# A two-layer hybrid trunk in fp32 on one core: the start reordered with small filler products, and the LRU gate products cut into 64x64 quarters

## What is computed

```python
for l in range(DEPTH):                         # DEPTH = 2
    xn = rmsnorm(x, pre_mix_g[l])
    u, g, q, k, v, gA, gB = split(xn @ w_in[l])
    # branch A: conv of width 4, then the gates of a linear recurrence
    uc = conv_b + sum(upad[:, k:k + S] * conv_w[k] for k in range(4))
    ub = uc.reshape(B, S, 16, 64)                              # 16 blocks of 64 channels
    r = sigmoid(einsum("bsnd,nde->bsne", ub, w_a) + b_a)       # a 64x64 matrix for each block
    i = sigmoid(einsum("bsnd,nde->bsne", ub, w_x) + b_x)
    h = scan(a=exp(-8 * r * softplus(-lam)), b=sqrt(1 - a*a) * i * uc)
    y_a = (h * gelu(g)) @ w_pa[l]
    # branch B: rotary, windowed attention with sinks, then @ w_pb[l]
    x = x + rmsnorm((sigmoid(gA) * y_a + sigmoid(gB) * y_b) @ w_o[l], post_mix_g[l])
    f = (silu(h @ w_ffn_gate[l]) * (h @ w_ffn_up[l])) @ w_ffn_down[l]    # h = rmsnorm(x, pre_ffn_g[l])
    x = x + rmsnorm(f, post_ffn_g[l])
```

## Time and profile before

| | |
|---|---|
| median of 3 runs | 822.87 us (822.86 to 823.91) |
| the profiled execution's own time | 823.39 us |
| span of its trace | 821.6 us |
| PE busy | 808.5 us, 98% of the span |
| DVE busy | 537.7 us, 65% |
| ACT busy | 419.5 us, 51% |
| POOL busy | 69.2 us, 8% |
| DMA | 148.07 MB, mean 180 GB/s |

### The profile page before, as it was taken

How to read it: one execution, slowest core, us unless ns; L and a number is a source line. 1 busy time by engine, 2 the same in 40 slices (tenths; PEclk the granted TensorE clock), 3 DMA queues, 4 the chain that set the end, 5 groups by cost and what they waited for, 6 DMA issues and landing times.

```text
span 821.6 us, 10326 instructions
## 1 busy us (share of the span) xinstructions
PE 808.5 (98%) x4221; PEld 683.9 (83%) x4221; DVE 537.7 (65%) x549; ACT 419.5 (51%) x543; POOL 69.2 (8%) x131
## 2 busy tenths in 40 slices
PE   7999999999999999999999999999999999999997
PEld 4898898888888888888879989988888888888885
DVE  5798898556666464545488869975467645645652
ACT  5556878633455343434345588865336434443431
POOL 7331000000120000000011300000003100000000
PEclk9999999999999999999999999999999999999999
DMA  9875545354358566654448735444454466655511
GB/s 280 262 256 157 160 162 184 119 184 164 108 200 279 175 213 204 198 164 151 154 132 274 276 131 186 155 154 154 158 199 153 169 218 208 201 179 187 198 52 51
DMA packets 80016, 148.07 MB, mean 180 GB/s; under 512 B 7137, under 2 KB 27745, under 8 KB 79970
## 3 DMA queue, kind: packets, MB, share of 16 engines
q1 hardware_dynamic: 79552, 147.40, 54.3%
q10 hardware_dynamic: 418, 0.02, 0.0%
HBM read 146.36 MB, written 1.05 MB: 179 GB/s over the span
## 4 chain that ended last, share of the span: by engine, by line
PE 97%; DVE 1%; DMA 1%; issue 0%; ACT 0%; POOL 0%; SPq 0%; DVEq 0%; POOLq 0%; ACTq 0%
PE work L636 17%; PE work L638 17%; PE work L637 17%; PE acc L636 9%; PE acc L638 9%; PE acc L637 9%; PE work L628 4%; PE work L630 4%; PE work L629 4%; PE work L770 1%; PE acc L701 1%; PE work L724 1%; DMA weights_raw<-in_w_in 1%; PE acc L714 1%; PE work L733 1%; PE work L734 1%
## 5 line engine op out<-in xcount | busy, mean ns | idle before, releaser
L1302 DVE TENSOR_TENSOR weights_lo<-weights_raw,weights_hi 128x2048 fp32r<-128x2048 f32 x132 | 301.7, 2290 | 156.1 <-ACT weights_hi L946 156.1
L946 ACT ACTIVATE weights_hi<-weights_raw 128x2048 fp32r<-128x2048 f32 x132 | 252.5, 1915 | 210.9 <-PE work L638 118.8
L636 PE MATMUL work<-weights_hi,act_a_hi 128*128 128x512 f32 x544 | 214.4, 394 | 0.0
L638 PE MATMUL work<-weights_hi,act_a_lo 128*128 128x512 f32 x544 | 212.1, 390 | 0.0
L637 PE MATMUL work<-weights_lo,act_a_hi 128*128 128x512 f32 x544 | 211.9, 389 | 0.0
L638 PEld LDWEIGHTS work<-weights_hi,act_a_lo 128*128 128x128 f32 x544 | 102.1, 188 | 21.4
L636 PEld LDWEIGHTS work<-weights_hi,act_a_hi 128*128 128x128 f32 x544 | 102.2, 188 | 21.0
L637 PEld LDWEIGHTS work<-weights_lo,act_a_hi 128*128 128x128 f32 x544 | 102.2, 188 | 20.5
L636 PE MATMUL acc<-weights_hi,act_b_hi 128*128 128x512 f32 x240 | 94.3, 393 | 0.0
L638 PE MATMUL acc<-weights_hi,act_b_lo 128*128 128x512 f32 x240 | 93.5, 390 | 0.0
L637 PE MATMUL acc<-weights_lo,act_b_hi 128*128 128x512 f32 x240 | 93.4, 389 | 0.0
(11 more groups left out here) (182 smaller groups left out, 895.9 us busy)
## 6 DMA issues: line engine op xcount, KB each, us to landing
weights_raw<-in_w_in SPq DMA_DIRECT2D x43, 1024.0 KB, 5.3
weights_raw<-in_w_ffn_down SPq DMA_DIRECT2D x22, 1024.0 KB, 4.9
weights_raw<-in_w_ffn_gate SPq DMA_DIRECT2D x20, 1024.0 KB, 5.2
weights_raw<-in_w_ffn_up SPq DMA_DIRECT2D x20, 1024.0 KB, 5.1
weights_raw<-in_w_pa SPq DMA_DIRECT2D x8, 1024.0 KB, 5.0
weights_raw<-in_w_pb SPq DMA_DIRECT2D x8, 1024.0 KB, 5.0
weights_raw<-in_w_o SPq DMA_DIRECT2D x8, 1024.0 KB, 4.8
weights_raw<-in_w_ffn_gate SPq DMA_DIRECT2D x4, 512.0 KB, 4.0
```

The costliest lines, as they stand in the source:

```text
L636: mm(dst, xh, wh, start=first, stop=False)
L638: return mm(dst, xl, wh, start=False, stop=final)
L946: activate(w_hi[:, SLOT[n], :], raw[:, n % RAW, :], ACT.Copy).then_inc(hi_done.sem, 1)
L1302: v.tensor_tensor(w_lo[:, SLOT[n], :], raw[:, n % RAW, :], bits(w_hi[:, SLOT[n], :]), ALU.subtract).then_inc(split_done.sem, 1)
```

## The change

The start: DVE's cast of the positions goes from the head of its order to a place behind the x tiles' work; the loads of positions and sinks go from ACT's queue to SP's, behind the third panel; ACT copies the turned x tile before it splits the second half of the first panel; POOL makes the second rstd right behind the first, ahead of the angle chain, and clears nothing; PE multiplies the identity by itself 5 times and 8 times (`keep_busy`), into a bank that nobody reads; the turning of `vec_rows` goes between two kv panel halves.

The gates: both 64x64 matrices of a block are stored side by side in `gate_w` (half the room, nothing to clear), and a group takes four fp32 products of 64 rows by 64 columns of weights, 256 columns moving. The r products of both halves go straight (rows b to output partitions b) into one bank, the i products crosswise into the other, so two groups share two banks. ACT reads r with one sigmoid for each group, i with two of 64 partitions, crosswise; `lru_bx` is loaded crosswise to fit.

```diff
@@ SP
-                                      lru_bx.rearrange("l (k b) e -> (l k) (b e)", b=2),
+                                      None,
+                    for b in range(2):
+                        sp.dma_start(vec_rows[row:row + DEPTH * KD, 64 - 64 * b:128 - 64 * b],
+                                     lru_bx.rearrange("l (k b) e -> b (l k) e", b=2)[b]).then_inc(rows_loaded, 16)
             load(0, 2)
+            sp.dma_start(pos_i[:, :], positions.rearrange("a (t p) -> p (a t)", p=P), ...
+            sp.dma_start(sink_rows[:, :, :], attn_sinks.rearrange("l h -> (l h)").partition_broadcast(P) ...
...
-                        sp.wait_ge(*cleared.at(l, 2))
+                        if not first:
+                            sp.wait_ge(*x_done.at(l - 1, 4))
@@ POOL
-            nc.gpsimd.memset(bd_a, 0.0).then_inc(cleared.sem, 1)
-            nc.gpsimd.memset(bd_x, 0.0).then_inc(cleared.sem, 1)
             steps[0] += 1
             rstd_of(0, (ms_done.sem, 1), steps[0])
+            steps[0] += 1
+            rstd_of(1, (ms_done.sem, 2), steps[0])
@@ PE
+            def keep_busy(n):
+                for _ in range(n):
+                    nc.tensor.transpose(work[3][:, 0:P], ident[:, :], ident[:, :])
+            keep_busy(WARM[0])
...
+            keep_busy(WARM[1])
@@ PE, gates
-                    for c in range(c0, c1):
-                        dst = claim(l, "gates", c)
-                        pe.wait_ge(*uc_done.at(l, c + 1))
-                        mm(dst[:, 0:S], bd_a[:, c, :], UC[:, c, :], start=True, stop=True)
-                        mm(dst[:, S:2 * S], bd_x[:, c, :], UC[:, c, :], start=True, stop=True
-                           ).then_inc(gates_mm.sem, 1)
+                    for pair in range(c0, c1, 2):
+                        dsts = [claim(l, "gates", c) for c in (pair, pair + 1)]
+                        pe.wait_ge(*uc_done.at(l, pair + 2))
+                        for c in (pair, pair + 1):
+                            cols = slice(S * (c - pair), S * (c - pair) + S)
+                            for i in range(2):
+                                for b in range(2):
+                                    rows = slice(64 * b, 64 * b + 64)
+                                    to = 64 * b if i == 0 else 64 - 64 * b
+                                    last = mm(dsts[i][to:to + 64, cols], gate_w[rows, c, 64 * i:64 * i + 64],
+                                              UC[rows, c, :], start=True, stop=True)
+                        last.then_inc(gates_mm.sem, 1)
@@ PE, first_products
-                    pe.wait_ge(rows_loaded, 16 * 5)
-                    nc.tensor.transpose(acc[:, 1, 0:P], vec_rows[:, :], ident[:, :]).then_inc(vec_turned, 1)
+                        if j == 0:
+                            pe.wait_ge(rows_loaded, 16 * 6)
+                            nc.tensor.transpose(acc[:, 1, 0:P], vec_rows[:, :], ident[:, :]).then_inc(vec_turned, 1)
@@ ACT
-            act.dma_start(pos_i[:, :], ...
-            act.dma_start(sink_rows[:, :, :], ...
             half_hi(0, 0).then_inc(head_hi, 1)
+            xa_hi(0, 0, "xn", 0)
             act.wait_ge(*raw_loaded[0].at(0, LOADED[0]))
             half_hi(0, 1).then_inc(hi_done.sem, 1)
-            xa_hi(0, 0, "xn", 0)
@@ DVE
-            dve.wait_ge(pos_loaded, 16)
-            v.tensor_copy(pos_f[:, :], pos_i[:, :]).then_inc(pos_done, 1)
...
-            xa_lo(0, 0, "xn", 0, range(1))
+            xa_lo(0, 0, "xn", 0)
             dve.wait_ge(*hi_done.at(0, 1))
             half_lo(0, 1).then_inc(split_done.sem, 1)
-            xa_lo(0, 0, "xn", 0, range(1, 2))
...
             xa_lo(0, 0, "xn", 1)
+            dve.wait_ge(pos_loaded, 16)
+            v.tensor_copy(pos_f[:, :], pos_i[:, :]).then_inc(pos_done, 1)
```

More of the change, by code:

```diff
@@ L40 @@
 GELU_SCALE = 0.7978845608028654
+WARM = (5, 8)
 RAW = 3
@@ L181, in trunk @@
         thA = QTOK
-        bd_a, bd_x = (QT[:, k:k + 4, :].rearrange("p a (b d) -> p (a b) d", b=2) for k in (0, 4))
+        gate_w = QT[:, 0:4, :].rearrange("p a (b d) -> p (a b) d", b=2)
         junk = KTOK[:, :, :, :].rearrange("p t g d -> p (t g d)")
@@ L413, in layer @@
                     if n == RAW:
[L415 removed]
+                        if not first:
+                            sp.wait_ge(*x_done.at(l - 1, 4))
                         for b in range(2):
[L417 to L418 removed]
+                            for i, src in enumerate((lru_wa, lru_wx)):
+                                sp.dma_start(gate_w[64 * b:64 * b + 64, :, 64 * i:64 * i + 64],
                                              src[l].rearrange("(k b) d e -> b d k e", b=2)[b]
[L420 removed]
+                                             ).then_inc(gate_w_loaded.sem, 16)
                     if n == 4 + RING + RAW:
@@ L531, in _ @@
                     less(n - m, 1 + m)
-                if n == 0:
-                    steps[0] += 1
-                    rstd_of(1, (ms_done.sem, 2), steps[0])
             for n, piece in ((2, 1), (1, 2), (0, 3), (2, 2), (1, 3), (2, 3)):
@@ L563, in layer @@
                         rstd_of(n, ms_done.at(l, m + 1), l * 10 + step)
-                if not last:
-                    pool.wait_ge(*x_done.at(l, 4))
-                    nc.gpsimd.memset(bd_a, 0.0).then_inc(cleared.sem, 1)
-                    nc.gpsimd.memset(bd_x, 0.0).then_inc(cleared.sem, 1)
             for_layers(pool, layer)
@@ L817, in layer @@
                 f_product("u", 1, xn_hi, xn_lo)
-                pe.wait_ge(*bd_loaded.at(l, 64))
+                pe.wait_ge(*gate_w_loaded.at(l, 64))
                 for j in range(2, 4):
@@ L1038, in gates @@
                 def gates(c0, c1):
-                    for c in range(c0, c1):
-                        act.wait_ge(*gates_mm.at(l, c + 1))
-                        ps = bank("gates", c)
-                        activate(h_lru[:, c, :], ps[:, 0:S], ACT.Sigmoid, bias=vec[:, 5, c:c + 1])
-                        done(activate(IG[:, c, :], ps[:, S:2 * S], ACT.Sigmoid, bias=vec[:, 6, c:c + 1]),
-                             gates_done, c + 1)
+                    for pair in range(c0, c1, 2):
+                        act.wait_ge(*gates_mm.at(l, pair // 2 + 1))
+                        for c in (pair, pair + 1):
+                            cols = slice(S * (c - pair), S * (c - pair) + S)
+                            ins = activate(h_lru[:, c, :], bank("gates", pair)[:, cols], ACT.Sigmoid,
+                                           bias=vec[:, 5, c:c + 1])
+                        done(ins, gates_done, pair + 1)
+                        for c in (pair, pair + 1):
+                            cols = slice(S * (c - pair), S * (c - pair) + S)
+                            for b in range(2):
+                                rows, at = slice(64 * b, 64 * b + 64), slice(64 - 64 * b, 128 - 64 * b)
+                                ins = activate(IG[rows, c, :], bank("gates", pair + 1)[at, cols], ACT.Sigmoid,
+                                               bias=vec[at, 6, c:c + 1])
+                        done(ins, gates_done, pair + 2)
                 def qk_copy(m0, m1):
```

18 lines of the change are left out of this document (8 added, 10 removed).

## The result

The changed kernel took 817.84 us (median of four runs, 817.29 to 818.09) against 822.87 for the kernel before, timed beside it (822.61 to 823.91). The recorded ratio is 0.9931, 95% interval 0.9919 to 0.9943; it is not the quotient of the two medians, which is 0.9939 and lies inside the interval. The span went from 821.6 to 816.3 us, 5.3 less, at a granted clock of 0.998.

What follows compares the result with a forecast made beforehand. PE, busy for 98% of the span, was taken as the bound. Start 2.2 plus gates 3.7 less 0.3 lost at DVE's third rope gave 5.6 us: 817.3 us, range 815.3 to 819.2 (chance 0.68), whole range up to 821.3.

Steps and rivals of the forecast that it cites:

- The gates: Eight gate calls: four quarters at once, 1.26 in place of 1.72 us a call, 3.7 us saved in all.
- The rival of two quarters at once: Gate calls: only two quarters run together, 2.13 us a call, a loss of 3.3; total 824.0, chance 0.12.
- The second tile: Start: second x tile normed earlier, so PE starts the second panel at 15.3 to 15.85, not 17.07; 1.5 us.
- The earlier landing of the second panel's first half: Start: the positions' 256 4-byte elements hold up the weights; moved away, that half may land 1.1 us earlier.
- The vectors: Start: turning the small vectors half a panel earlier hides DVE's copies behind PE's work; 0.7 us saved.
- The start in sum: Second tile 1.5 plus vectors 0.7: 2.2 us saved, bounds 1.2 and 2.8.
- The fillers: Start: 5 and 8 extra PE products; without an earlier higher clock level they cost 0.55 of slack.
- The lower clock level: Start: PE at 1.2, not 2.4 GHz, 0.21 us a pass.
- What the gain runs into: Before q1 in layer 0: PE, 3.1 us earlier, meets 2.4 of slack at DVE's third rope; 0.3 lost.
- POOL's angle chain: Layer 0: angle steps take 20.7 us and end at about 38.5, before DVE asks at about 44.
- the angles come late: Layer 0: positions landing at 23 or later hold back ropes, then q1; 2 us late gives 819.3, chance 0.05.

Runs made afterwards that it cites:

- run 2: Only the gate products in quarters, with the start of the kernel before; 819.66 us, ratio 0.9949.
- after: The changed kernel with the whole change, against the kernel before; 817.84 us, ratio 0.9931.
- run 5: Changed kernel with r and i of each row half in one bank of its own, ACT reading both gates in halves; 820.59 us, ratio 0.9955.
- run 6: Changed kernel with POOL casting the positions itself in place of DVE; 817.51 us, ratio 0.9923.
- run 7: Changed kernel with the gate products in another order, both groups on one quarter before the next quarter; 817.43 us, ratio 0.9927.
- run 10: Kernel of run 9 with eight more fillers ahead of the gain row's spread; 817.95 us, ratio 0.9932.
- run 8: Changed kernel with only the sinks' load put back on ACT's queue, behind the gain row; 818.36 us, ratio 0.9933.
- run 3: Changed kernel with no filler products; 817.43 us, ratio 0.9927.
- run 9: Changed kernel with POOL casting the positions, and DVE doing decay rates before panel 4's split, sinks and vectors before panel 5's; 816.93 us, ratio 0.9922.
- run 4: Changed kernel with the loads of positions and sinks put back on ACT's queue at the start; 818.03 us, ratio 0.9933.

## Why the prediction was right, and where it was not

The total came out at 817.84 where 817.3 was said, by terms of which some were off.

**The gates: right in mechanism, a little small in size.** Four quarters run at once, in four steps of 0.216. The term was 0.46 a call and measured 0.50 (run 2, and six calls of after): getting in and out costs 0.36, not the 0.40 read from the scores. 4.0 instead of 3.7. The rival of two quarters at once is excluded by the starts, and run 5 shows why nothing of it came: in time, a bank shared by row parts on different partitions is no obstacle. By the rule of the Trainium skill, TensorEngine Tiling (Array Packing), Restrictions and Gotchas, that different row tiles can't access the same PSUM bank at the same time, run 5 should have been quicker at each call; it was not (1.22 both ways).

**The second tile: mis-sized, 1.02 for 1.5,** and below the 1.2 to 1.8 that was given for it. The step that failed is "DVE norms the first tile as soon as rstd is there, at about 6.25". The norm came at 7.10, by two things. The x tile landed later in this execution (ACT squared from 4.47, before from 4.12), so rstd was there at 6.60 and not at 6.18. And the norm has a second operand, the spread gain row: PE needs 3.75 for the spread, and the row landed at 3.31, at 2.22 in the trace that was read. Everything behind the norm moved with it: first product 11.22 for 9.95 to 10.5, second panel 16.05 for 15.3 to 15.85. Where the row landed at 2.21 (runs 6 and 7) the norm came at 6.38, the first product at 10.51 and the second panel at 15.17, so the rest of the step's sum holds. The x tile goes with the row: ACT squares from 4.10 to 4.19 in the six traces with an early row and from 4.21 to 4.75 in the six with a late one (run 10 hides its row behind the fillers), and no edit here decides which it is.

The earlier landing of the second panel's first half was right, too, but not its reason. The sum had the 256 elements of 4 bytes of the positions hold up the weights; run 8, with the sinks' load alone back on ACT's queue, has the same dip and the same late landing.

**The vectors: 0.77 for 0.7.** The start in sum: 1.77 for 2.2, within its bounds.

**The fillers** cost the first product 0.6 (run 3, less the row's 0.3) and give back more by the clock, 0.42 at the second panel (run 3); in the total this is masked. "The lower clock level" is read from spacings here, 0.43 for a product against 0.23, 0.21 for a pass against 0.11: the granted clock that the profile prints is 1.00 for the whole start, before and after.

**What the gain runs into: size right, cause right in part.** 0.40 was lost in the first two calls of layer 0 for the 0.3 said. The cause given was DVE's own work from the split of u panel 1 on. Three things meet at q1, and the traces tell which came last (starts and ends in us; PE's own way from the second panel to q1 takes 44.65 without a wait, as runs 3 and 9 show):

| kernel | second panel | u panel 1: ACT rounds from | POOL's angles end | DVE starts on them | waited for POOL | q1 | q1 less second panel |
|---|---|---|---|---|---|---|---|
| after | 16.05 | 28.91 | 43.81 | 43.85 | 0.67 | 61.13 | 45.08 |
| run 3 | 16.47 | 27.33 | 43.29 | 43.33 | 1.53 | 61.12 | 44.65 |
| run 4 | 15.82 | 29.97 | 39.70 | 44.24 | none | 61.33 | 45.51 |
| run 6 | 15.18 | 29.46 | 37.40 | 43.60 | none | 60.67 | 45.50 |
| run 7 | 15.17 | 28.16 | 43.04 | 43.07 | 0.67 | 60.23 | 45.06 |
| run 8 | 16.24 | 30.05 | 39.83 | 44.37 | none | 61.46 | 45.22 |
| run 9 | 15.95 | 28.68 | 42.41 | 42.45 | 1.95 | 60.60 | 44.65 |

In after it was POOL's angle chain. It was put at 20.7 and took 25.3, because its steps fell beside six full splits; it ended at 43.81 for 38.5, and DVE waited 0.67 for it. That is the rival "the angles come late", in part and by another cause than the one named: the positions landed in time (15.3), the steps were slow. In runs 4, 6 and 8 it was the cause that the prediction gave: DVE comes to the angles 14.1 to 14.3 after ACT begins to round u panel 1, and that panel landed late. Without its wait for POOL after's DVE would have come there at 43.18, 14.27 behind that landing: the two chains lie 0.67 apart. Run 9 takes DVE's own work out of the way and PE runs free, though DVE waits 1.95 for POOL.

What moves u panel 1 is open. SP issues its load when DVE has split panel 2, at 20.8 in after and 21.5 in run 3, and ACT rounds it 8.1 and 5.8 later; in runs 4, 6 and 8 that takes 9.0 to 9.5. No experiment changes that load by itself, so that q1 starts anywhere from 60.23 to 61.46 in these kernels is in part the luck of the landings.

Why the steps were slow: the row shows POOL's step beside a split as long as the split. The Trainium skill, SBUF — State Buffer, Who interferes with whom, says that a DVE instruction with two SBUF inputs contends with a GpSimd instruction that reads SBUF, and that this contention is an exclusive lock. The splits have two such inputs, and the trace agrees, with 2.1 to 2.5 for steps of 0.25 to 0.4. No run here took the second input away, so the port as the cause is not shown by an experiment.

In sum: 1.77 + 4.0 - 0.40 = 5.4, the span's 5.3.

## What to carry to other kernels

Block-diagonal products of 64x64 are worth cutting by rows: two row halves beside each other cost half the steps and some 0.4 us for each excursion, so call them for as many blocks at once as are ready; cut the columns too only if it puts the results where another engine can read them whole. When a start is made earlier, look for the chains that do not move with it: here a string of small POOL steps, whose price depends on what DVE does beside them and which was costed from a time with other neighbours, and a panel load that lands when it lands. They lay within a us of each other, so taking one away alone won nothing (run 6). Compare only traces whose start fell alike. And list every operand of a step before saying when it begins; the one that was never late before may be the last to come now.

## What the runs showed of the hardware

- POOL's 128x64 steps take 0.25 to 0.4 us alone and 2.1 to 2.5 us beside a 128x2048 subtraction of two tiles on DVE, one slow step for each such subtraction; they moved with it when it was moved (run 9).
- With the load of the sinks on ACT's queue among the first loads the DMA moves 70 to 106 GB/s in the slice from 5 to 6 us, without it 233 to 381 (before and runs 2, 4 and 8 against the other nine traces). In run 8 the 256 elements of 4 bytes of the positions were elsewhere.
- Four passes of 64x64 products start within 0.02 us, and within 0.04 when two products are queued for each quarter in a row (run 7).
- A sigmoid over 64 partitions by 256 takes 0.48, as over 128 (run 5).
- A load of 4 KB, the first on its queue, landed at 2.2 to 2.4 in half of the traces and at 3.0 to 3.6 in the others. That is 0.9 us of the start, and no edit here explains it.
- PE went at its lower clock level, by the spacing of its passes, until 10.1 to 12.9 us with the 13 fillers (nine traces) and until 15.4 to 15.9 without (before and runs 2 and 3); eight more fillers from 1.74 on did not bring the rise forward (run 10).
